# Out projections of a four-mixer block: from one fp32 product to three passes of split operands

## The chip, the cores and the metric

The kernel runs on one core of one Trainium2 chip. The metric is device microseconds of one execution. Three executions of the kernel before gave 1533.09, 1534.29 and 1536.28 us, a median of 1534.29 us.

## What is computed

The input is a sequence of 256 tokens with 1024 features. It runs through eight phases, each of the form x = x + f(rmsnorm(x)):

- **even**: a projection of 3584 columns, a causal depthwise convolution of 31 taps with layer norm and silu (features 0 to 511 of y), and softmax attention with 8 heads (features 512 to 1023 of y);
- **odd**: a projection, compressed, selected and windowed attention with gates (y 0 to 511) and sliding-window attention with sinks (y 512 to 1023);
- twice **ffn1, mix, ffn2**: a SwiGLU network with 2816 hidden features, a mixer, and another SwiGLU network. The mixer has an RWKV-7 recurrence with a group norm (y 0 to 511) and a chunked retention (y 512 to 1023).

Even, odd and the two mixers end with the same step, the subject of this document:

```python
x = x + einsum('bse,ed->bsd', y, w_out[layer])      # y: 256 x 1024, w_out: 1024 x 1024
# the end of the mixer's first half, ahead of that step
y = (y - mean) * rsqrt(var + LN_X_EPS) * ln_w + ln_b
y = (y + sum(r_h * k_h * r_k) * v_h) * g
```

## The kernel before, in words

**Tiles and passes.** All weights come as one stream of tiles of 128 x 1024 fp32 (512 KB), in the order of use, into a ring of six slots (`weight_ring`). A tile is either 128 columns of a weight over all 1024 inputs, or 128 rows of it (a row tile). The projections and the SwiGLU phases don't multiply in fp32: each operand a is split into hi = a rounded to fp32r (a copy on ScalarE, ACT) and lo = a - hi (a subtraction on VectorE, DVE). Then `three_passes` (L698 to L703) adds the products hi·hi, hi·lo and lo·hi in PSUM. `down` (L1009) does the same with row tiles, on the shape 128x128 by 128x512.

**The out projection** (L805, `out_projection`) is the exception: it takes y (`yT`, 128 features by 256 tokens for each of 8 groups k) and a row tile straight from the ring, and multiplies in fp32 at L815. For each of the eight row tiles it issues four matmuls of 128x128 by 128x512, one for each 128 tokens and each half of the 1024 output columns. They add up in PSUM banks 0 to 3. When the eighth is done, `add_to_x` (L1788) adds the four banks to x.

**Its inputs.** Attention phases make y in pairs of heads: `pair_done` on DVE (L1878 even, L1972 and L1975 odd) writes one group of `yT`, under the semaphore `pair_out`. The even phase's other half comes from the convolution: sums over features on TensorE (PE, L842 and L847), the centring (L1880), the square, the inverse root (L1400, L1401), a scaling (L1883), silu (L1458) and a product (L1885). In the mixer, the retention's half of y is written long before the end, and the recurrence's half last: group-norm sums (L1304, L1313), inverse root, then L2213, four scalings by ln_w and ln_b (L2215), the bonus (L2218) and the gate (L2219). The function `y_wait` holds PE in front of the group k that isn't made yet. The even phase and the mixer go through the groups 4 to 7 first and then 0 to 3; the odd phase goes through 0 to 7.

**What sets the order.** There is no planner: each engine (PE, ACT, DVE, and SP for the DMAs) has its own program, written out by hand in program order, and semaphores tie them together. An instruction that waits holds everything behind it on its engine. `attention` exists on all three engines with one step s for each pair of heads, plus some steps at the end to drain; `hook(s)` is where other work is put between the parts of a step. `ahead(n + 1)` (ACT L1363 ff., DVE L1766 ff.) splits the first two tiles of the next phase while the out projection runs. SP loads tile t + 6 into the slot of tile t as soon as that is free: after the lo part of a split tile is made (L618 ff.), or after PE's last matmul on an unsplit one (semaphore `w_used`, L625).

**Memory.** `arena` is scratch that shares its addresses with the hi and lo operands: six places for weight tiles (`w_hi`, `w_lo`), and `hT_hi`, `hT_lo`, the phase's normalised input. These are idle once a phase's last projection job is done.

## Time and profile before

| | |
|---|---|
| median of the runs | 1534.29 us (1533.09 to 1536.28) |
| the profiled execution, its own time | 1535.23 us |
| its span in the profile | 1533.4 us |
| PE busy | 1441.1 us, 94% of the span |
| DVE busy | 847.9 us, 55% |
| ACT busy | 689.1 us, 45% |
| matmuls of the out projections (L815) | 111.1 us of the busy time |
| mean granted clock of TensorE | 0.967 |

The profiled execution took 1535.23 us and its span is 1533.4 us, so 1.8 us lie around the span. A busy share says how full an engine is, not that it bounds: for that one reads, stage by stage, which wait ends last. A matmul's duration in a row (592 ns for L815) is its latency through a pipeline. What a run of matmuls costs is read from the time between its first and its last. One fp32 matmul leaves two records, so the 128 matmuls of L815 stand as 256.

### The profile page before, as it was taken

The numbers are of one execution on the slowest core, as the hardware profiler recorded it, in microseconds if no ns is written. First come the engines' busy times: TensorE is split into PE (matmuls) and PEld (weight loads), VectorE is DVE, ScalarE is ACT, GpSimd is POOL, SyncE is SP. The second block draws the span as 40 slices with busy tenths as digits, with TensorE's granted clock in tenths as the row PEclk, the third lists the DMA queues.
The fourth block names the chain that finished last, engine by engine and source line by source line (L and its number), as shares of the span: only waits on it lengthen the run. The fifth ranks groups of instructions, "written<-read, shape, count | busy, mean of one in ns | idle before, by whom it ended". The sixth has DMA issues, their size and how long they took to land.

```text
span 1533.4 us, 29116 instructions
## 1 busy us (share of the span) xinstructions
PE 1441.1 (94%) x11842; PEld 1264.9 (82%) x11842; DVE 847.9 (55%) x1218; ACT 689.1 (45%) x1044; POOL 9.9 (1%) x23
## 2 busy tenths in 40 slices
PE   6986997889999999999999999999999999999998
PEld 6974586665999989987599998999989988499997
DVE  4966526654555566744554546555557745455454
ACT  5452536554444446621444445444455531344443
POOL 1000000000000000000000000000000000000000
PEclk9996998899999999989999999999999989999999
DMA  8620544106655554400565554555545400465551
GB/s 328 207 83 18 189 167 176 56 1 195 202 178 194 175 167 163 138 3 3 165 208 188 182 187 152 204 186 183 189 154 168 150 15 3 150 207 177 192 179 67
DMA packets 62061, 228.14 MB, mean 149 GB/s; under 512 B 6928, under 2 KB 6928, under 8 KB 61728
## 3 DMA queue, kind: packets, MB, share of 16 engines
q1 hardware_dynamic: 60048, 218.14, 42.6%
q0 software_dynamic: 1936, 8.89, 1.7%
q8 instruction: 59, 0.97, 0.3%
q14 instruction: 18, 0.15, 0.0%
HBM read 225.95 MB, written 1.05 MB: 148 GB/s over the span
## 4 chain that ended last, share of the span: by engine, by line
PE 87%; DVE 5%; ACT 5%; issue 1%; DMA 1%; DVEq 0%; SPq 0%; ACTq 0%; PEldq 0%
PE PS L702 52%; PE PS L1009 15%; PE PS L815 7%; ACT arena L1347 1%; DVE w_lo L1764 1%; PE PS L1164 1%; PE PS L1196 1%; PE PS L1202 1%; PE PS L1211 1%; DVE arena L1857 1%; PE PS L1146 1%; PE PS L801 1%; PE PS L1141 1%; DVE x_res L1788 1%; DVE arena L1810 1%
## 5 line engine op out<-in xcount | busy, mean ns | idle before, releaser
L702 PE MATMUL PS<-hT_hi,w_hi 128*128 128x256 f32 x2136 | 612.2, 287 | 16.9 <-DVE w_lo L1764 10.6
L702 PE MATMUL PS<-hT_lo,w_hi 128*128 128x256 f32 x2136 | 608.7, 285 | 0.0
L702 PE MATMUL PS<-hT_hi,w_lo 128*128 128x256 f32 x2136 | 608.5, 285 | 0.0
L702 PEld LDWEIGHTS PS<-hT_hi,w_hi 128*128 128x128 f32 x2136 | 414.3, 194 | 24.8 <-issue 21.3
L702 PEld LDWEIGHTS PS<-hT_lo,w_hi 128*128 128x128 f32 x2136 | 414.3, 194 | 3.9 <-issue 0.7
L702 PEld LDWEIGHTS PS<-hT_hi,w_lo 128*128 128x128 f32 x2136 | 414.1, 194 | 0.0
L1984 DVE TENSOR_TENSOR w_lo<-weight_ring,w_hi 128x1024 fp32r<-128x1024 f32 x176 | 207.5, 1220 | 30.0 <-ACT w_hi L1548 30.0
L1990 DVE TENSOR_TENSOR w_lo<-weight_ring,w_hi 128x1024 fp32r<-128x1024 f32 x88 | 107.9, 1226 | 166.0 <-ACT w_hi L1557 166.0
L1548 ACT ACTIVATE w_hi<-weight_ring 128x1024 fp32r<-128x1024 f32 x176 | 175.6, 1044 | 39.5 <-DMA weight_ring<-in_stream 39.5
L1764 DVE TENSOR_TENSOR w_lo<-weight_ring,w_hi 128x1024 fp32r<-128x1024 f32 x107 | 126.1, 1221 | 54.6 <-ACT w_hi L1371 54.3
L1557 ACT ACTIVATE w_hi<-weight_ring 128x1024 fp32r<-128x1024 f32 x88 | 93.2, 1059 | 113.1 <-PE PS L1009 113.1
L1585 ACT ACTIVATE silu_gate<-PS 128x256 f32<-128x256 f32 x88 | 33.8, 384 | 239.3 <-PE PS L702 239.3
L1009 PE MATMUL PS<-w_hi,act_hi 128*128 128x512 f32 x352 | 138.0, 392 | 0.0
L1009 PE MATMUL PS<-w_hi,act_lo 128*128 128x512 f32 x352 | 138.0, 392 | 0.0
L1009 PE MATMUL PS<-w_lo,act_hi 128*128 128x512 f32 x352 | 136.9, 389 | 0.0
L2002 DVE TENSOR_TENSOR ffn_act<-silu_gate,PS 128x256 f32<-128x256 f32 x88 | 37.1, 422 | 143.7 <-ACT silu_gate L1585 143.7
L1371 ACT ACTIVATE w_hi<-weight_ring 128x1024 fp32r<-128x1024 f32 x107 | 107.1, 1052 | 18.6 <-DMA weight_ring<-in_stream 18.6
L815 PE MATMUL PS<-weight_ring,yT 128*128 128x512 f32 x256 | 111.1, 592 | 0.6 <-issue 0.6
L815 PEld LDWEIGHTS PS<-weight_ring,yT 128*128 128x128 f32 x256 | 48.7, 191 | 61.1 <-issue 60.9
L1009 PEld LDWEIGHTS PS<-w_lo,act_hi 128*128 128x128 f32 x352 | 66.1, 188 | 14.4
L1009 PEld LDWEIGHTS PS<-w_hi,act_hi 128*128 128x128 f32 x352 | 66.4, 189 | 11.6
L1009 PEld LDWEIGHTS PS<-w_hi,act_lo 128*128 128x128 f32 x352 | 66.4, 189 | 10.5
(275 smaller groups left out, 1353.3 us busy)
## 6 DMA issues: line engine op xcount, KB each, us to landing
weight_ring<-in_stream SPq DMA_DIRECT2D x411, 512.0 KB, 4.4
norm_gain<-in_gains_in POOLq DMA_DIRECT2D x9, 512.0 KB, 5.2
consts<-in_csts POOLq DMA_DIRECT2D x1, 1864.0 KB, 10.2
arena<-in_bias_in POOLq DMA_DIRECT2D x1, 1152.0 KB, 13.0
x_res<-in_x_in SPq DMA_DIRECT2D x2, 512.0 KB, 3.9
lora<-in_lora_in POOLq DMA_DIRECT2D x2, 512.0 KB, 5.7
x_out<-yT SPq DMA_DIRECT2D x2, 512.0 KB, 2.7
params<-in_params SPq DMA_DIRECT2D x1, 260.5 KB, 7.2
```

Source lines behind the costliest of these rows:

```text
L702: ins = pe.matmul(out, w[a], x[b], start=(start and i == 0), stop=(stop and i == 2))
L801: ins = pe.transpose(PS[:, 6 + e, c * P:(c + 1) * P], S[:, (s - 1) % 3, e, c * P:(c + 1) * P], ident)
L815: ins = pe.matmul(PS[:, 2 * t + half, :], YT[:, k, t * P:(t + 1) * P], w[:, half * 512:(half + 1) * 512], start=(i == 0), stop=(i == 7))
L1009: ins = pe.matmul(o, (Ah, Al)[x][:, s, t * P:(t + 1) * P], w[y][:, cols], start=(start and j == 0), stop=(stop and j == 2))
L1371: act.activation(Wh[:, q % RING], Wr[:, tile % NSLOT], ACT.Copy).then_inc(sem("tile_hi"), 1)
L1548: act.activation(Wh[:, 3 * (i % SS) + part], Wr[:, t % NSLOT], ACT.Copy)\
L1557: act.activation(Wh[:, 3 * (i % SS) + 2], Wr[:, t % NSLOT], ACT.Copy)\
L1585: act.activation(sg[:, s, :], PS[:, 4 + s, 0:T], ACT.Silu).then_inc(sem("silu_made"), 1)
L1764: dve.tensor_tensor(Wl[:, q % RING], Wr[:, tile % NSLOT], Wh[:, q % RING], ALU.subtract)\
L1984: dve.tensor_tensor(Wl[:, u], Wr[:, (tile0 + 3 * i + part) % NSLOT], Wh[:, u], ALU.subtract)\
L1990: dve.tensor_tensor(Wl[:, u], Wr[:, (tile0 + 3 * i + 2) % NSLOT], Wh[:, u], ALU.subtract)\
L2002: dve.tensor_tensor(aT[:, s, :], sg[:, s, :], PS[:, 4 + s, T:2 * T], ALU.mult)\
```

## The change

There are three parts.

1. **Three passes.** The out projection calls `three_passes` with y as the stationary and the row tile as the moving operand. New functions make the operands: `row_hi` (ACT, 128x1024) and `row_lo` (DVE, 128x1024) for a row tile, `y_hi` (ACT) and `y_lo` (DVE) for a group of y of 128x256 or 128x512. The split row tiles have two pairs of places (`OW[0][:, i % 2]`, `OW[1][:, i % 2]`), so `row_hi` of row i waits until PE is done with row i - 2 (`row_used`). The places lie where `w_lo` 4 and 5, `hT_hi` and `hT_lo` were; `yT_lo` lies on `yT` itself.
2. **Order.** `row_hi` and `row_lo`, `y_hi` and `y_lo` are written into the programs of ACT and DVE: rows 0 and 1 in the attention hooks (even, odd) or ahead of the last chain (mixer), rows 2 to 5 between the steps of the last chain, rows 6 and 7 behind the next phase's two split tiles. A ring slot of a row tile is free when its lo part is made, no longer after the matmuls. The odd phase takes the groups 4 to 7 first, as the others do.
3. **Last chains in halves.** In the even phase silu and the product are signalled and made in two halves. In the mixer ln_w, ln_b, the bonus and the gate are folded early into two factors (`output_factors`, in the inversion loop), and the last chain is three operations for each half of the features instead of seven for all of them.

```diff
...
-    return u + row_tiles(paired(wo[:512], 0), range(4)) + row_tiles(paired(wo[512:], 0), range(4)), 45
+    return u + row_tiles(paired(wo[512:], 0), range(4)) + row_tiles(paired(wo[:512], 0), range(4)), 45
...
-WOUT = {"even": (28, EVEN_OUT), "odd": (35, list(range(8))), "mix": (26, [4, 5, 6, 7, 0, 1, 2, 3])}
+WOUT = {"even": (28, EVEN_OUT), "odd": (35, EVEN_OUT), "mix": (26, EVEN_OUT)}
+Y_GROUPS = {"even": [(4, 5), (5, 6), (6, 7), (7, 8), (0, 2), (2, 4)], "odd": [(4, 6), (6, 8), (0, 1), (1, 2), (2, 3), (3, 4)],
+            "mix": [(4, 6), (6, 8), (0, 2), (2, 4)]}
...
+def outs_before(n):
+    kinds = [p[0] for p in PHASES[:n] if p[0] in WOUT]
+    return len(kinds), sum(len(Y_GROUPS[k]) for k in kinds)
...
+        with nc.sbuf_tensor("yT_lo", [P, KT, T], F32R) as YL:
+            pass
         YT = sb("yT", KT, T)
...
+        with nc.sbuf_tensor("out_operands", [P, ARENA], F32R) as rounded:
...
+        OUT_AT = PROJ_END - 6 * D
+        YH = rounded[:, OUT_AT:OUT_AT + KT * T].rearrange("p (k t) -> p k t", k=KT)
+        OW = [rounded[:, OUT_AT + 2 * D * (1 + i):OUT_AT + 2 * D * (2 + i)].rearrange("p (r n) -> p r n", r=2) for i in range(2)]
...
-                    else:
+                    elif i < WOUT[kind][0]:
                         used += 1
                         sp.wait_ge(sem("w_used"), used)
+                    else:
+                        sp.wait_ge(sem("row_lo"), 8 * outs_before(n)[0] + i - WOUT[kind][0] + 1)
...
-                first, order = WOUT[kind]
-                base = tile0 + first
-                for i, k in enumerate(order):
+                outs, groups = outs_before(n)
+                for i, k in enumerate(WOUT[kind][1]):
                     y_wait(k)
-                    tile_ready(base + i)
-                    w = unit(base + i).rearrange("p a b -> p (a b)")
+                    g = [a <= k < b for a, b in Y_GROUPS[kind]].index(True)
+                    pe.wait_ge(sem("y_lo"), groups + g + 1)
+                    pe.wait_ge(sem("row_lo"), 8 * outs + i + 1)
                     for t in range(NTT):
+                        y = [a[:, k, t * P:(t + 1) * P] for a in (YH, YL)]
                         for half in range(2):
-                            ins = pe.matmul(PS[:, 2 * t + half, :], YT[:, k, t * P:(t + 1) * P],
-                                            w[:, half * 512:(half + 1) * 512], start=(i == 0), stop=(i == 7))
+                            w = [a[:, i % 2, half * 512:(half + 1) * 512] for a in OW]
+                            ins = three_passes(PS[:, 2 * t + half, :], y, w, i == 0, i == 7)
                             if i == 7:
                                 ins.then_inc(sem("acc_made"), 1)
-                    if i < 7:
-                        ins.then_inc(sem("w_used"), 1)
-                pe.wait_ge(sem("acc_made"), 4 * n + 4)
-                pe.sem_inc(sem("w_used"), 1)
...
-                    if k == 0:
-                        pe.wait_ge(sem("y_conv_made"), 1)
...
+            def row_hi(n, i):
+                kind, l, tile0 = PHASES[n][:3]
+                tile = tile0 + WOUT[kind][0] + i
+                act.wait_ge(*loaded(tile))
+                if i >= 2:
+                    act.wait_ge(sem("row_used"), 6 * outs_before(n)[0] + i - 1)
+                act.activation(OW[0][:, i % 2], slot_of(tile), ACT.Copy).then_inc(sem("row_hi"), 1)
+            def y_hi(n, g):
+                lo, hi = Y_GROUPS[PHASES[n][0]][g]
+                act.activation(YH[:, lo:hi, :], YT[:, lo:hi, :], ACT.Copy).then_inc(sem("y_hi"), 1)
...
-                attention("even", lambda s: None)
+                attention("even", lambda s: row_hi(ph, s - 3) if s >= 3 else None)
+                for g in range(4):
+                    act.wait_ge(sem("pair_out"), g + 1)
+                    y_hi(ph, g)
                 act.wait_ge(sem("conv_centred"), 1)
                 act.activation(flat(convsq), flat(conv), ACT.Square).then_inc(sem("convsq_made"), 1)
+                row_hi(ph, 2)
                 act.wait_ge(sem("ln_sum_made"), 2)
                 inv_root(lnrs, PS[:, 4, T:2 * T], 1.0 / 512).then_inc(sem("lnrs_made"), 1)
+                row_hi(ph, 3)
+                act.preload_act_table(ACT.Silu)
                 act.wait_ge(sem("conv_scaled"), 1)
                 for c in range(4):
                     ins = act.activation(conv[:, c, :], conv[:, c, :], ACT.Silu, scale=par("a_ln_g", c, 1),
                                          bias=par("a_ln_b", c, 1))
-                ins.then_inc(sem("conv_act"), 1)
-            def odd_layer(jb0, hn0):
+                    if c % 2:
+                        ins.then_inc(sem("conv_act"), 1)
+                row_hi(ph, 4)
+                for h in range(2):
+                    act.wait_ge(sem("y_conv_made"), h + 1)
+                    y_hi(ph, 4 + h)
...
+                    elif s in (10, 11):
+                        row_hi(ph, s - 10)
...
                 attention("odd", hook)
+                act.wait_ge(sem("y_swa_made"), 1)
+                y_hi(ph, 0)
+                y_hi(ph, 1)
+                for j in range(4):
+                    act.wait_ge(sem("pair_out"), 4 + 4 + j + 1)
+                    y_hi(ph, 2 + j)
+                for i in range(2, 5):
+                    row_hi(ph, i)
...
+                row_hi(ph, 0)
+                for g in range(2):
+                    act.wait_ge(sem("y_ret_made"), 2 * l + 2)
+                    y_hi(ph, g)
+                row_hi(ph, 1)
...
+                row_hi(ph, 2)
                 act.wait_ge(sem("gn_sum"), 2 * l + 2)
                 inv_root(flat(aS), banks(6), 1.0 / HD, cst("lneps")).then_inc(sem("gn_rs_made"), 1)
+                row_hi(ph, 3)
+                row_hi(ph, 4)
+                for h in range(2):
+                    act.wait_ge(sem("y_mix_made"), 2 * l + h + 1)
+                    y_hi(ph, 2 + h)
...
+                    row_hi(n, 5)
                     ahead(n + 1)
+                    row_hi(n, 6)
+                    row_hi(n, 7)
...
+            def row_lo(n, i):
+                kind, l, tile0 = PHASES[n][:3]
+                dve.wait_ge(sem("row_hi"), 8 * outs_before(n)[0] + i + 1)
+                dve.tensor_tensor(OW[1][:, i % 2], slot_of(tile0 + WOUT[kind][0] + i), OW[0][:, i % 2], ALU.subtract)\
+                   .then_inc(sem("row_lo"), 1)
+            def y_lo(n, g):
+                lo, hi = Y_GROUPS[PHASES[n][0]][g]
+                dve.wait_ge(sem("y_hi"), outs_before(n)[1] + g + 1)
+                dve.tensor_tensor(YL[:, lo:hi, :], YT[:, lo:hi, :], YH[:, lo:hi, :], ALU.subtract)\
+                   .then_inc(sem("y_lo"), 1)
...
+                def with_rows(s):
+                    hook(s)
+                    if s >= 5:
+                        row_lo(ph, s - 5)
+                attention("even", lambda c, pv: dve.tensor_tensor(YT[:, c.tile, :], pv, ZB[:, c.j, :], ALU.mult), with_rows)
+                for g in range(4):
+                    y_lo(ph, g)
                 dve.wait_ge(sem("ln_sum_made"), 1)
                 dve.scalar_tensor_tensor(conv, rep(PS[:, 4, 0:T], 4), -1.0 / 512, conv, ALU.mult, ALU.add)\
                    .then_inc(sem("conv_centred"), 1)
+                row_lo(ph, 2)
                 dve.wait_ge(sem("lnrs_made"), 1)
                 dve.tensor_tensor(conv, conv, rep(lnrs, 4), ALU.mult).then_inc(sem("conv_scaled"), 1)
-                dve.wait_ge(sem("conv_act"), 1)
-                dve.tensor_tensor(YT[:, 0:4, :], conv, ZA, ALU.mult).then_inc(sem("y_conv_made"), 1)
-            def odd_layer(jb0, hn0):
+                row_lo(ph, 3)
+                for h in range(2):
+                    dve.wait_ge(sem("conv_act"), h + 1)
+                    cc = slice(2 * h, 2 * h + 2)
+                    dve.tensor_tensor(YT[:, cc, :], conv[:, cc, :], ZA[:, cc, :], ALU.mult)\
+                       .then_inc(sem("y_conv_made"), 1)
+                row_lo(ph, 4)
+                for h in range(2):
+                    y_lo(ph, 4 + h)
...
+                    elif s in (11, 12):
+                        row_lo(ph, s - 11)
                     elif s == 13:
                         dve.wait_ge(sem("z_gated"), 2)
                         dve.wait_ge(sem("pair_out"), 4 + 4)
-                        dve.tensor_tensor(flat(YT[:, 4:8, :]), flat(YT[:, 4:8, :]), flat(ZB), ALU.mult)
+                        dve.tensor_tensor(flat(YT[:, 4:8, :]), flat(YT[:, 4:8, :]), flat(ZB), ALU.mult)\
+                           .then_inc(sem("y_swa_made"), 1)
+                    elif s == 14:
+                        y_lo(ph, 0)
+                        y_lo(ph, 1)
...
+                for j in range(4):
+                    y_lo(ph, 2 + j)
+                for i in range(2, 5):
+                    row_lo(ph, i)
...
+                def output_factors(j):
+                    dve.wait_ge(sem("bonus_made"), l + 1)
+                    dve.wait_ge(sem("g_copied"), l + 1)
+                    dve.scalar_tensor_tensor(vS[:, j, :], vS[:, j, :], p_("ln_b", j), gS[:, j, :], ALU.add, ALU.mult)
+                    dve.tensor_scalar(gS[:, j, :], gS[:, j, :], p_("ln_w", j), None, ALU.mult)\
+                       .then_inc(sem("factors_made"), 1)
...
+                    if s < 4:
+                        output_factors(s)
...
+                row_lo(ph, 0)
+                y_lo(ph, 0)
+                y_lo(ph, 1)
...
+                row_lo(ph, 1)
+                row_lo(ph, 2)
+                dve.wait_ge(sem("factors_made"), 4 * l + 4)
                 dve.wait_ge(sem("gn_rs_made"), l + 1)
-                done.wait(done(dve.tensor_tensor(flat(Yl), flat(Yl), flat(aS), ALU.mult)))
-                for j in range(4):
-                    k = done(dve.tensor_scalar(Yl[:, j, :], Yl[:, j, :], p_("ln_w", j), p_("ln_b", j),
-                                               ALU.mult, ALU.add))
-                done.wait(k)
-                done.wait(done(dve.tensor_tensor(flat(Yl), flat(Yl), flat(vS), ALU.add)))
-                dve.tensor_tensor(flat(YT[:, 0:4, :]), flat(Yl), flat(gS), ALU.mult).then_inc(sem("y_mix_made"), 1)
+                for h in range(2):
+                    hh = slice(2 * h, 2 * h + 2)
+                    y = flat(Yl[:, hh, :])
+                    done.wait(done(dve.tensor_tensor(y, y, flat(aS[:, hh, :]), ALU.mult)))
+                    done.wait(done(dve.tensor_tensor(y, y, flat(gS[:, hh, :]), ALU.mult)))
+                    dve.tensor_tensor(flat(YT[:, hh, :]), y, flat(vS[:, hh, :]), ALU.add)\
+                       .then_inc(sem("y_mix_made"), 1)
+                    row_lo(ph, 3 + h)
+                for h in range(2):
+                    y_lo(ph, 2 + h)
...
+                    row_lo(n, 5)
                     ahead(n + 1)
+                    row_lo(n, 6)
+                    row_lo(n, 7)
```

## Rows read from the trace of the kernel before

**Rows 1.** The page: busy time of TensorE, and the chain by line.
```profile
PE 1441.1 (94%) x11842; PEld 1264.9 (82%) x11842; DVE 847.9 (55%) x1218; ACT 689.1 (45%) x1044; POOL 9.9 (1%) x23
...
PE PS L702 52%; PE PS L1009 15%; PE PS L815 7%; ACT arena L1347 1%; DVE w_lo L1764 1%; PE PS L1164 1%; PE PS L1196 1%; PE PS L1202 1%; PE PS L1211 1%; DVE arena L1857 1%; PE PS L1146 1%; PE PS L801 1%; PE PS L1141 1%; DVE x_res L1788 1%; DV
```

**Rows 2.** The chain in order of time: start, length, what.
```profile
268.00 1.75 ACT arena L1420 x8
...
333.10 1.04 DVE arena L1833 x2
...
340.97 26.00 PE PS L815 x60
...
385.90 2.75 PE PS L1009 x12
```

**Rows 3.** Windows: busy us of PE, PEld, DVE, ACT, POOL; granted clock; DMA.
```profile
141.00:145.00 4.00, 3.91 (x9) 3.09 (x10) 0.13 (x2) 0.00 (x0) 0.00 (x0) 0.53 0.00 0
...
298.00:302.00 4.00, 1.49 (x16) 0.77 (x14) 3.72 (x16) 0.47 (x1) 0.00 (x0) 0.97 0.78 260
302.00:305.00 3.00, 2.83 (x14) 2.50 (x16) 2.86 (x9) 1.25 (x4) 0.00 (x0) 0.50 0.02 8
...
337.00:341.00 4.00, 1.97 (x19) 1.16 (x17) 1.65 (x2) 1.96 (x3) 0.00 (x0) 1.00 0.00 0
...
341.00:368.70 27.70, 27.67 (x64) 12.02 (x64) 4.53 (x5) 4.38 (x5) 0.00 (x0) 1.00 0.43 133
```

**Rows 4.** Timeline of the first mixer's end: PE, then ACT, then DVE.
```profile
727.78 1.88 PE L1313 MATMUL PS<-arena,consts 128*128 128x512 f32 x4
729.50 24.20 PE L815 MATMUL PS<-weight_ring,yT 128*128 128x512 f32 x56
...
718.59 1.09 ACT L1706 ACTIVATE arena<-PS 128x512 f32<-128x512 f32 x2 [11.73 <-PE PS L1271]
...
729.70 1.11 ACT L1400 ACTIVATE arena<-PS,consts 128x1024 f32<-128x1024 f32 x1 [2.83 <-PE PS L1313]
...
740.15 1.06 ACT L1548 ACTIVATE w_hi<-weight_ring 128x1024 fp32r<-128x1024 f32 x1 [8.24 <-DMA weight_ring<-in_stream]
...
752.74 1.06 ACT L1347 ACTIVATE arena<-x_res 128x1024 f32<-128x1024 f32 x1 [6.79 <-DVE x_res L1788]
...
716.76 0.68 DVE L2180 TENSOR_TENSOR arena<-PS,arena 128x512 f32<-128x512 f32 x1
721.46 1.02 DVE L2207 TENSOR_TENSOR arena<-arena,PS 128x384 f32<-128x384 f32 x2 [4.02 <-PE PS L1298]
...
733.20 1.38 DVE L2215 TENSOR_SCALAR arena<-arena,params 128x256 f32<-128x256 f32 x4
...
735.88 1.23 DVE L2219 TENSOR_TENSOR yT<-arena 128x1024 f32<-128x1024 f32 x1
...
753.74 0.69 DVE L1788 SCALAR_TENSOR_TENSOR x_res<-PS,x_res 128x512 f32<-128x512 f32 x1 [0.17 <-PE PS L815]
```

**Rows 5.** Timeline of the second mixer's inversion loop, DVE.
```profile
1265.09 0.42 DVE L2160 TENSOR_TENSOR arena<-arena,PS 128x256 f32<-128x256 f32 x1 [0.75 <-PE PS L1211]
```

**Rows 6.** Timeline of the odd phase's last attention steps: ACT, then DVE.
```profile
331.38 0.81 ACT L1428 ACTIVATE lora<-PS 128x768 f32<-128x768 f32 x1
...
337.21 1.06 ACT L1536 ACTIVATE arena<-arena 128x1024 f32<-128x1024 f32 x1
338.18 0.79 ACT L1428 ACTIVATE lora<-PS 128x768 f32<-128x768 f32 x1
...
340.44 0.42 DVE L1975 TENSOR_TENSOR yT<-PS,arena 128x256 f32<-128x256 f32 x1 [0.91 <-PE PS L784]
```

**Rows 7.** Timeline of the even phase's end: PE, DVE and ACT.
```profile
140.61 0.42 DVE L1878 TENSOR_TENSOR yT<-PS,arena 128x256 f32<-128x256 f32 x1 [0.26 <-PE PS L776]
141.09 3.78 PE L842 MATMUL PS<-arena,consts 128*128 128x256 f32 x8 [0.53 <-DVE yT L1878]
...
155.74 2.07 ACT L1458 ACTIVATE arena<-arena,params 128x256 f32<-128x256 f32 x4
```

38 lines of the change are left out of this document (19 added, 19 removed).

## The prediction, made before the run

> **What bounds the kernel now.** I read the page first. TensorE is busy for 1441 of 1533 us, and the chain that ended last lies on it, with 7% in L815, the out projection's fp32 matmuls [rows 1]. A full engine proves nothing by itself, so next came the chain in order of time, around one out projection: 60 records without a gap in 26.00 us [rows 2]. PE bounds that stage, and less work on PE shortens it, as long as the work is fed. The windows give the clock: 1.00 over the odd phase's out projection, so the 2.4 GHz level [rows 3]. Last I read the timelines of the stage's three engines around it, since the change moves work to ACT and DVE.
>
> **The gross gain.** A fp32 matmul costs two records of 26.00/60 = 0.433 us, and a row tile (4 matmuls) 3.47 us, 8 of them 27.7 us. That is also the odd window of 27.70 us with 64 records [rows 2, 3]. Three passes of 128x128 by 128x512 in fp32r are what L1009 does: 12 matmuls in 2.75 us, 0.229 each [rows 2]. A row tile then costs 2.75 us and eight cost 22.0 us. So PE saves 5.7 us in each of the four out projections, 22.9 us in all. Now what eats into it.
>
> Beside the trace, the Trainium skill, FP8 and Floating Point Precision (TensorE Precision Notes), says that true fp32 takes four passes through the array. By that alone three passes would be 3/4 of 27.7, an estimate of 20.8 us. The row of L1009 gives 22.0, and it goes into the sum.
>
> **The feed.** Each row tile now needs an ACT copy (1.06 us, as the hi copy at 740.15) and then a DVE operation of 1.23 us (128x1024, as L2219) [rows 4]. A handover costs 0.04 us: L1313 ends at 729.66 and ACT starts at 729.70 [rows 4]. With two pairs of places, row i+2 is ready 1.06 + 1.23 + 3 x 0.04 = 2.4 us after row i is done, and row i+1 covers 2.75 us. It fits by 0.35 us, if ACT and DVE do nothing else. So each phase has to be followed in program order.
>
> **The mixer (twice).** Rows 0 and 1 and the retention's y: ACT is idle 11.73 us ahead of 718.59 and needs 2 x 1.06 + 2 x 0.55 = 3.2 us there. DVE's `row_lo(0)` and two `y_lo` (0.68 each, as L2180) take 2.6 us from 717.44 to 720.0. DVE is idle 4.02 us there, until 721.46 [rows 4]. Cost: nothing. Row 0 on PE starts at 724.35, as now (eight records of 0.43 ahead of 727.78), and ends at 727.1. The sums L1313 (1.88) run to 729.0 instead of 729.66. ACT's `row_hi(2)` fits ahead of them (727.1 to 728.2). Row 1 ends at 731.7, and row 2, whose lo is ready at 729.5, at 734.5. ACT's inverse root (two operations, 2.2 us) ends at 731.2. DVE then does half a chain (3 x 0.69 = 2.1, to 733.3) and `row_lo(3)` to 734.6: row 3 runs 734.65 to 737.4, a stall of 0.15. Then come the second half to 736.7, `row_lo(4)` to 737.9 and `y_lo(2)` to 738.6. Row 4 can't start before 738.65: a stall of 1.25. From there PE is continuous: DVE needs 1.23 for row 5, 2.46 for the next phase's two tiles and 1.23 for row 6 (739.3 to 744.15), and row 6 is due at 744.15. The next phase's tiles are loaded in time. Now the hi copy waits for a DMA until 740.15, whose slot came free with row 2 at 736.4 (3.75 us before); after the change it comes free with `row_lo(2)` and `row_lo(3)`, at 729.5 and 734.6. Row 7 ends at 749.65, against 753.70 (729.50 + 24.20) now [rows 4]: 4.05 us earlier.
>
> The tail gives some back. The four banks finish 0.69 us apart instead of 0.87, and the adds take 0.69 each. The second add, for which ACT's first square waits, now ends 0.96 us ahead of PE's end (752.74 against 753.70). It will end 0.6 ahead. The last add ends as late after PE's end as it does now, 0.73 us (753.74 + 0.69), but ACT's two token tiles follow each other without a gap, so the next phase starts 0.36 us later against PE's end [rows 4]. Four times: 1.4 us.
>
> `output_factors` adds a 128x256 operation with three inputs (0.42) and one of 1.38/4 = 0.35 [rows 4, 5] in each of four rounds of the inversion loop. DVE is idle 0.75 us there [rows 5], so 0.77 us hides but for some 0.02 to 0.1 us. I take 0.15 us for each mixer; without that cover it would be 4 x 0.77 = 3.1. The chain gets shorter by the four scalings and the half that is signalled early, but `y_mix_made` is at 737.1 now and PE wants group 0 at 739.8 (729.50 + 24 x 0.43) [rows 4]: that gain is spent on the feed.
>
> Each mixer: 4.05 - 0.36 - 0.15 = 3.55 us. Two: 7.1 us.
>
> **The odd phase.** The hooks of steps 10 and 11 put `row_hi` ahead of the PT copy (331.38) and `row_lo` ahead of the normalisation on DVE [rows 6]. ACT: `row_hi(0)` to 332.4, the PT copy to 333.25, the exponentials of step 11 (eight records, 1.75 and a handover [rows 2]) to 335.1, `row_hi(1)` to 336.15. At step 12 DVE waits for that, does `row_lo(1)` to 337.4 and normalises (1.04 [rows 2] behind three small operations of some 0.2) to 339.0, and PE transposes (0.9) to 339.95. ACT's last PT copy slips from 338.18 to 339.95 (now it waits for the silu from 337.21). Then the two `y_lo` of step 14 stand ahead of the last `pair_done`: it ends at about 343.1 instead of 340.86, and PE's row 0 starts at 343.2 instead of 340.97, 2.2 us late [rows 2, 6]. The rows then run continuously but for 0.55 at row 6: behind `row_lo(5)` (356.55), DVE has the two tiles (359.0) and `row_lo(6)` (360.2), and row 6 is due at 359.7. End: 343.2 + 22.0 + 0.55 = 365.75 against 368.7. Less the tail: 2.95 - 0.36 = 2.6 us gained.
>
> **The even phase.** Here the last `pair_done` on DVE is what PE waits for, until 141.09 [rows 7]. `row_lo(0)` and `row_lo(1)` come in steps 5 and 6, ahead of the last two `pair_done`: 2 x 1.23, less 0.26 of idle, puts it at 143.15 and L842 at 143.2, 2.1 us late. L842 takes 3.78 us, rows 0 and 1 end at 152.5, the second sums (8 records of half that size at the full clock, 1.89) at 154.4, row 2 at 157.15. Inverse root, `row_hi(3)`, the table load and the wait for the scaling bring silu to 157.7 instead of 155.74. `row_lo(3)` is ready at 157.9: a stall of 0.75. silu (2.07) ends at 159.8, then `row_hi(4)`, `row_lo(4)` and `y_lo(4)` to 162.85: a stall of 2.2. End at 173.9 against 174.06. With the tail, the even phase loses 0.2 us.
>
> **The sum.** 7.1 + 2.6 - 0.2 = 9.5 us. The profiled execution took 1535.23 us, so 1525.7 by it; it lies 0.94 us above the median of 1534.29. The change applied to the median gives **1524.8 us**.
>
> **What the trace of before doesn't show.** (1) A DVE subtraction or an ACT copy that reads the ring beside fp32r matmuls of 512 columns: L1009's stage does that, so no loss; at the other end 10% more on 1.23 and 1.06 would use 0.23 of the 0.35 us of margin. (2) The handover through three engines in each row: 0.04 each by the row above, up to 0.2 (the gap of DVE behind L815 is 0.17 [rows 4]), so a row between 2.75 and 2.9 us: 0 to 24 x 0.15 = 3.6 us lost. I take 0, since 0.35 of margin stands against it. (3) The clock.
>
> **Rivals.**
>
> *The clock falls at the start of row 0.* Between 298 and 302 PE was busy for 1.49 of 4 us, with its work at the front, and the next window was granted 0.50, the 1.2 GHz level; 337 to 341, with 1.97 of 4, kept 1.00 [rows 3]. After the change the last steps of the odd phase are stretched, with about 3.5 us busy in 8 and gaps near 1 us. In the even phase L842 already runs at the low level (0.53), behind a gap that grows from 0.53 to 2.6 us. If one row runs at the low level it costs 2.75 us more; in both phases 5.5: 1527.5 to 1530.3. For it: the gaps grow. Against it: none of the odd phase's is as long as the 2.5 us in which PE was idle in that window.
> The Trainium skill, TensorE: Matmul & The Clock Gate (Part 1), says that half rate is the idle state and that sustained activity lifts it. By that rule the even phase's row 0 still starts at the full clock, since L842 runs ahead of it; the trace agrees.
>
> *The feed sets the pace, and the kernel gets slower.* Place: `row_lo` behind `row_hi` behind `row_used`, 32 rows. If a row takes p instead of 2.75 us, the loss is 32(p - 2.75), which eats the 9.5 us at p = 3.05, a chain of 2.4 us lengthened by 0.65. At p = 3.3, 17.6 us are lost and the time is 1542. For it: the margin of 0.35, and ACT and DVE have other work between the rows in every phase. Against it: the durations of both are read in the SwiGLU stage, where they run as densely.
>
> *The hidden gain.* The late starts cost more than I worked out: the even and the odd phase lose 3 us each beyond it (one more `row_lo` plus one stall of 2 us), and each mixer's stall at row 4 is 2.5. Then 1533. For it: the four delays add up through three engines. Against it: every step has its row.
>
> *It doesn't do what it says.* Nothing in the diff leaves the fp32 path in place, so no chance for that.
>
> **Chances.** Forecast 1524.8 (1521 to 1528): 0.60. Clock: 0.17. Hidden gain: 0.13. Feed, slower: 0.10. What a measurement can tell from no change is about 0.2%, 3.1 us. Faster by more than that: 0.60 + 0.17 and a little of the hidden gain, 0.80. Same: 0.12. Slower: 0.08. The range that holds 8 in 10 reaches from 1520.5, with shorter stalls at row 4, to 1531, through most of the clock's case.
>
> **What would show it.** L815's place taken by 384 fp32r matmuls in L702's helper, 12 in 2.75 us. In each mixer one PE stall of about 1.2 us ahead of group 0, waited for by `y_lo`, and the end 4 us earlier. In the odd phase row 0 late by 2.2 us; in the even phase L842 at about 2.1 us late, with the end where it was. ACT's square 0.6 ahead of PE's end. Wrong would be: rows more than 2.85 us apart without a step of the last chain between them (the feed), a granted clock under 0.9 within an out projection, or an inversion loop over 1 us longer.

## The result, and the profile after

| | before | after | ratio (95% interval) |
|---|---|---|---|
| first comparison, median of 4 runs each | 1534.03 us (1533.09 to 1536.28) | 1525.46 us (1523.79 to 1527.44) | 0.9947 (0.9926 to 0.9968) |
| same kernel again, 6 runs (18 of before) | 1534.32 us | 1524.73 us (1523.66 to 1526.84) | 0.9942 (0.9927 to 0.9956) |

The forecast was 1524.8 us, faster by 9.5. The change is worth 8.6 and 9.6 us in the two comparisons. The profiled execution took 1526.04 us (span 1524.3).

The page after: busy time of the engines, the chain that ended last by engine, and the group of out projection matmuls with both operands in `out_operands`.

```profile
PE 1422.4 (93%) x11970; PEld 1288.3 (85%) x11970; DVE 898.0 (59%) x1285; ACT 729.9 (48%) x1096; POOL 9.9 (1%) x23
...
PE 84%; DVE 8%; ACT 5%; issue 1%; DMA 1%; DVEq 0%; SPq 0%; ACTq 0%; PEldq 0%
...
L719 PE MATMUL PS<-out_operands 128*128 128x512 f32 x256 | 84.0, 409 | 6.1 <-DVE yT_lo L1851 3.0
```

TensorE is busy 18.7 us less [rows 1] and the span is 9.1 us shorter; VectorE is busy 50 us more, and its share of the chain has gone from 5 to 8%. That fits a change that takes work off the bound and pays half of it back in waits. The waits can be read one by one. The timeline of PE around the out projections, only the lines with an idle time ahead: even phase, odd phase, first mixer.

```profile
143.59 2.93 PE L858 MATMUL PS<-arena,consts 128*128 128x256 f32 x6 [2.44 <-DVE yT L1955]
...
158.91 0.70 PE L719 MATMUL PS<-out_operands 128*128 128x512 f32 x2 [0.74 <-DVE out_operands L1844]
...
163.58 0.73 PE L719 MATMUL PS<-out_operands 128*128 128x512 f32 x2 [1.67 <-DVE yT_lo L1851]
...
344.14 0.70 PE L719 MATMUL PS<-out_operands 128*128 128x512 f32 x2 [1.45 <-DVE yT L2068]
...
361.46 0.70 PE L719 MATMUL PS<-out_operands 128*128 128x512 f32 x2 [0.40 <-DVE out_operands L1844]
...
735.81 0.70 PE L719 MATMUL PS<-out_operands 128*128 128x512 f32 x2 [0.23 <-DVE out_operands L1844]
739.50 0.73 PE L719 MATMUL PS<-out_operands 128*128 128x512 f32 x2 [0.69 <-DVE yT_lo L1851]
```

Every stall that the prediction named is there. It had put 2.1 us ahead of the even phase's first sums (L858, L842 before [rows 7]), 0.75 and 2.2 behind it, 0.55 at row 6 of the odd phase, 0.15 and 1.25 in the mixer. Only their sizes differ.

The chain in order of time through the odd phase's out projection (start, length, what):

```profile
341.74 0.64 ACT out_operands L1395
342.38 0.02 issue
342.41 0.56 DVE yT_lo L1851
342.96 0.06 issue
343.02 0.68 DVE yT_lo L1851
343.70 0.35 DVE yT L2068
344.05 0.09 issue
344.14 11.37 PE PS L719 x48
355.50 0.02 issue
355.52 0.02 ACTq L1390
355.54 0.04 issue
355.59 1.07 ACT out_operands L1391
356.65 0.02 issue
356.68 1.23 DVE out_operands L1844
357.90 2.27 DVE w_lo L2081 x2
360.17 1.15 DVE out_operands L1844
361.32 0.14 issue
361.46 3.71 PE PS L719 x15
```

Its upper part is what holds row 0: two low parts of y on VectorE (L1851) ahead of the last normalised pair (L2068). Its lower part holds row 6: the next phase's two tiles (L2081) ahead of row 6's low part. The granted clock is 1.00 through this stretch of the odd phase, the 2.4 GHz level [rows 3]:

```profile
337.00:341.00 4.00, 1.98 (x17) 1.12 (x14) 3.31 (x8) 3.62 (x4) 0.00 (x0) 1.00 0.53 179
341.00:345.00 4.00, 2.17 (x16) 1.46 (x17) 3.30 (x8) 2.82 (x7) 0.00 (x0) 1.00 0.00 0
345.00:367.00 22.00, 21.61 (x94) 16.80 (x92) 11.72 (x13) 9.81 (x10) 0.00 (x0) 1.00 0.48 153
```

In the even phase it is lower. There row 0 starts at 146.81, and the clock is at 0.50 (the 1.2 GHz level) until 148.95:

```profile
144.00:147.00 3.00, 3.00 (x9) 2.37 (x8) 0.87 (x3) 0.00 (x0) 0.00 (x0) 0.50 0.71 232
147.00:149.00 2.00, 2.00 (x6) 1.52 (x6) 1.22 (x1) 0.33 (x1) 0.00 (x0) 0.51 0.04 16
149.00:152.00 3.00, 3.00 (x15) 2.45 (x14) 0.00 (x0) 1.71 (x2) 0.00 (x0) 1.00 0.00 0
```

In the kernel before, row 0 starts at 144.66 and the clock rises at 144.74. The first mixer's row 0 has 1.6 us at 0.50 too (724.23 to 725.81).

### The profile page after: what moved, and what is told of

It reads as the page before. It is cut to its first block, busy times and chain, and to the rows that moved or that the text cites. A ratio compares the mean times of both kernels' runs of the same rounds, so it can differ in the third digit from the quotient of the medians.

```text
span 1524.3 us, 29548 instructions
## 1 busy us (share of the span) xinstructions
PE 1422.4 (93%) x11970; PEld 1288.3 (85%) x11970; DVE 898.0 (59%) x1285; ACT 729.9 (48%) x1096; POOL 9.9 (1%) x23
## 3 DMA queue, kind: packets, MB, share of 16 engines
HBM read 225.95 MB, written 1.05 MB: 149 GB/s over the span
## 4 chain that ended last, share of the span: by engine, by line
PE 84%; DVE 8%; ACT 5%; issue 1%; DMA 1%; DVEq 0%; SPq 0%; ACTq 0%; PEldq 0%
PE PS L719 56%; PE PS L1023 15%; ACT arena L1357 1%; DVE w_lo L1822 1%; PE PS L707 1%; DVE arena L1928 1%; PE PS L1178 1%; PE PS L1210 1%; PE PS L1216 1%; DVE out_operands L1844 1%; DVE x_res L1859 1%; PE PS L1160 1%; PE PS L781 1%; DVE arena L1881 1%; PE PS L1155 1%
## 5 line engine op out<-in xcount | busy, mean ns | idle before, releaser
L2081 DVE TENSOR_TENSOR w_lo<-weight_ring,w_hi 128x1024 fp32r<-128x1024 f32 x176 | 207.3, 1220 | 0.0
L719 PE MATMUL PS<-out_operands 128*128 128x512 f32 x256 | 84.0, 409 | 6.1 <-DVE yT_lo L1851 3.0
L719 PEld LDWEIGHTS PS<-out_operands 128*128 128x128 f32 x256 | 47.6, 191 | 23.2 <-issue 9.3
```

Of the source, the lines that this page charges most:

```text
L719: ins = pe.matmul(out, w[a], x[b], start=(start and i == 0), stop=(stop and i == 2))
L2081: dve.tensor_tensor(Wl[:, u], Wr[:, (tile0 + 3 * i + part) % NSLOT], Wh[:, u], ALU.subtract)\
```

## The experiments

**Which part of the change brings it.** The first kernel is the one before with the mixers' part of the shorter chains alone:

```
+ output_factors(s) in rounds 0 to 3 of the inversion loop
- y = Yl * aS (128x1024); Yl * gS; + vS;  y_mix_made once
+ for h in range(2): the three operations on a half; y_mix_made twice
```

> The kernel before with the third part of the change alone, in the mixers: output_factors in the inversion loop, and the last chain in halves with two signals. Fp32 out projection as before. Theory: the chain was hidden (y_mix_made at 737.1 against a need at 739.8) and the factors hide in DVE's 0.75 us of idle, so 1534.3, between 0.5 less and 1 more. Rival: the shorter chain carries part of the measured gain by itself, 1532 or less. Second rival: the factors stand in the way of the inversion loop, 4 x 0.77 us in each mixer, 1540.

Measured: 1534.71 us (12 runs), ratio 0.9996 (0.998 to 1.0012). The mixers' chain alone gives nothing that can be measured: a shorter chain beside a busy PE is hidden. The gain is the split matmuls' (or needs them). The even phase's halves weren't tried alone.

**The changed kernel again**, as the base of the comparisons:

> The changed kernel once more, for a narrower interval and a second trace. My reading of its first trace: the out projections and their starts gained what was worked out (mixers about 3.2 us each of the expected 3.55, even phase +0.5 instead of +0.2, odd phase 2.4 instead of 2.6), while two stretches at the 1.2 GHz level moved: one came in at the start of the first SwiGLU phase (1.9 us lost, row 0 there took 5.75 + 1.9 us), one fell away at the start of the second mixer (1.7 us gained). If these come by chance, this trace shows them at other phase starts, and the median stays at 1525.5 (1524 to 1527). Rival: the change itself moved the clock (longer gaps ahead of the first SwiGLU phase), then the same two places show it again.

Measured: 1524.73 us (1523.66 to 1526.84, 6 runs), as expected. Of the two places, the start of the first SwiGLU phase is low in the second trace again, and that of the second mixer, which was low for 3.4 us only in the first trace, is low for 6.8 us. So one place speaks for the rival, that the change itself moved the clock, and one for chance. The count over all traces (below) bears on it.

**The work on rows 0 and 1 ahead of the attention's last steps.** It is moved behind them, or to where PE doesn't wait:

```
- even: row_lo(0), row_lo(1) in steps 5 and 6      + behind the attention
- odd, ACT: row_hi(0), row_hi(1) in steps 10, 11   + step 9; between the two y_hi
- odd, DVE: row_lo in steps 11, 12; y_lo(0), y_lo(1) in step 14
+ row_lo(0) in step 13; y_lo(0), row_lo(1), y_lo(1) behind the attention
```

> The changed kernel, with the row tiles' and y's splits moved behind the last pair in the even and odd phases: row_lo(0), row_lo(1) after the attention on DVE in the even phase; in the odd phase row_hi(0) in step 9, row_lo(0) in step 13, row_hi(1), row_lo(1) and the first two y_lo after the last pair_done. Theory: the late starts of L858 (2.0 us) and of row 0 (2.4 us) were these operations standing ahead of pair_done, so 4.4 us come back: 1521.1 (1520 to 1522.5). Rival (hidden): the work only moves and row 0 or row 1 waits for it instead; then 1525.

Measured: 1518.57 us (1516.99 to 1521.8), ratio 0.9898 (0.9882 to 0.9915), 6.2 us less than the changed kernel and 1.4 below the range expected. In the even phase L858 starts 2.07 us behind the start of the last attention step's matmuls (L793), as in the kernel before; in the changed kernel it was 3.99. So 1.9 us of the even phase's delay is the two low parts. In the odd phase I count from the fourth-last step's matmuls of PT (the tile `lora`) to row 0: 11.3 us before, 13.4 after, 12.0 here. The gain in medians is larger than these 1.9 + 1.4 us. Another 0.7 is in the even phase's rows 0 and 1: up to the second sums they take 6.0 us for 6.7, since the clock is at 0.50 for the first 0.5 us of them and not for 2.1. The other 2.2 aren't shown to be the change's. The even phase's stretch from its first normed operation to row 0 is 130.2 us here and 134.0 to 134.2 in four traces with the changed kernel's code, but 132.1 in three others with the same code ahead of row 0, so they may be scatter.

**The next phase's tiles between rows 6 and 7.** Both engines do one of the two tiles ahead of row 6 and one behind it (`ahead(n + 1, 0)`, row 6, `ahead(n + 1, 1)`, row 7).

> The changed kernel, with the next phase's two split tiles put one behind row 5 and one behind row 6, instead of both between 5 and 6. Theory: only the odd phase's row 6 has a stall there (0.4 us), so 1525.1, no more than 0.7 less than the changed kernel. Rival (feed sets the pace in rows 5 to 7 of every phase): 2 to 4 us less.

Measured: 1526.37 us (1516.93 to 1529.77, 7 runs), ratio 0.9943 (0.992 to 0.9965): no difference. The stall at row 6 of the odd phase is gone (its rows take 22.5 us for 23.1), but 0.6 us is under the scatter.

**Is the feed hidden, and by how much?** Three kernels ask it. The first leaves one pass out of each product, which makes the rows cheaper for PE while the feed stays:

```
- three_passes(PS[...], y, w, i == 0, i == 7)
+ for m, (a, b) in enumerate(((0, 0), (0, 1))): pe.matmul(PS[...], y[a], w[b], ...)
```

> The changed kernel with two of the three passes of each out projection product: y high by row high and y high by row low; the third, y low by row high, is left out, and with it that part of the product (y low is still made and waited for). A row tile then costs TensorE 8 instead of 12 matmuls, 2.75 x 8/12 = 1.83 us, 0.92 us less; four projections of 8 rows make 29.3 us of TensorE work less. My theory, corrected after the first traces: the chain that feeds a row (row high copy 1.06 us, row low subtraction 1.22 us, and the handovers, about 2.2 to 2.6 us a row with two pairs of places) is just under 2.75 us, so that it is hidden now and becomes the bound as soon as the rows are cheaper: rows 2 to 7 then take 2.3 to 2.6 us each instead of 1.83, and a projection saves 2 x 0.92 for its first two rows and at most 6 x 0.4 for the rest, less what the late groups of y hold (even and mixers nothing before row 4): some 2 to 4 us a projection, 8 to 16 in all: 1510 to 1517 us. Rival 1, TensorE alone sets the pace: 29 us less, 1496. Rival 2, the feed sets the pace already in the changed kernel: nothing is saved behind row 1, about 1522 to 1525, and the rows of the trace stand 2.75 us apart as before.

Measured: 1521.73 us (1517.63 to 1523.5), ratio 0.9927 (0.9905 to 0.9948). 29.3 us of PE's work left the kernel and only 3 us of time. The time is above the 1510 to 1517 expected and next to the second rival's 1522; the distance of the rows, 2.32 us for that rival's 2.75, speaks against it. The timeline of PE in its odd phase, rows 0 and 1, then 2 and 3, then 4 and 5:

```profile
341.22 3.89 PE L835 MATMUL PS<-out_operands 128*128 128x512 f32 x16 [1.44 <-DVE yT L2070]
345.87 3.91 PE L835 MATMUL PS<-out_operands 128*128 128x512 f32 x16 [0.75 <-DVE out_operands L1846]
350.50 3.91 PE L835 MATMUL PS<-out_operands 128*128 128x512 f32 x16 [0.73 <-DVE out_operands L1846]
```

ScalarE and VectorE in the same timeline:

```profile
348.04 1.06 ACT L1393 ACTIVATE out_operands<-weight_ring 128x1024 fp32r<-128x1024 f32 x1 [1.77 <-PE PS L835]
349.13 1.23 DVE L1846 TENSOR_TENSOR out_operands<-weight_ring,out_operands 128x1024 fp32r<-128x1024 f32 x1 [1.60 <-ACT out_operands L1393]
```

Two rows every 4.64 us, and PE waits ahead of each pair. Half of the pair's 3.9 us is row 2, so by this estimate it ends at 347.82; ScalarE starts row 4 0.22 behind it and takes 1.06; VectorE starts at 349.13, takes 1.23, and PE starts 0.14 later: 2.68 us (4.64 - 1.95 = 2.69). Neither engine is full: both stand idle for over 1.5 us ahead of these rows. What binds is the cycle of a place, with two places.

The third pair of places tests that. `OUT_AT` moves down by two row tiles, `i % 2` becomes `i % 3`, and row i waits for the matmuls of row i - 3:

```
- OUT_AT = PROJ_END - 6 * D              + OUT_AT = PROJ_END - 8 * D
- act.wait_ge(row_used, 6 * outs + i - 1)  + act.wait_ge(row_used, 5 * outs + i - 2)
```

> The kernel with two passes (y low by row high left out of the product) and three pairs of places instead of two. My theory: what held the rows of the two-pass kernel at 2.32 us is the cycle of a place (copy, subtraction, handovers, matmuls), not ScalarE or VectorE (1.06 and 1.22 us a row): with three places that cycle gives (2.69 + 1.95) / 3 = 1.55 us a row, below the 1.95 of the matmuls, so the odd phase's rows 2 to 7 stand 1.95 us apart; up to 0.37 x 6 = 2.2 us less there than with two pairs, 1 us in the other phases, where the rest waits for the late groups of y: 1517 us beside 1521.7. Rival, the engines' own queues (the copy and the subtraction in turn, other work between them) set 2.32 us: no change in the pitch, 1521.7.

Measured: 1517.17 us (1511.0 to 1519.28), ratio 0.9893 (0.9877 to 0.9909), 4.6 us less than two passes with two pairs. ScalarE's copies of rows 3 to 5 in the odd phase now stand 1.93 and 1.81 us apart, at the pace of PE; the waits behind each pair are gone:

```profile
340.58 1.06 ACT L1393 ACTIVATE out_operands<-weight_ring 128x1024 fp32r<-128x1024 f32 x1 [2.55 <-PE PS L835]
342.51 1.06 ACT L1393 ACTIVATE out_operands<-weight_ring 128x1024 fp32r<-128x1024 f32 x1 [0.86 <-PE PS L835]
344.32 1.06 ACT L1393 ACTIVATE out_operands<-weight_ring 128x1024 fp32r<-128x1024 f32 x1 [0.75 <-PE PS L835]
```

Shown, then: the cycle of the two places set 2.32 us, not an engine's queue. The third kernel comes from the other side and lengthens the feed of the full three passes: the low part of rows 2 to 7 is made twice. An earlier forecast for it, made for a first form that gave no result, was 3.4 us a row and 1541 us (1536 to 1546).

> The changed kernel with VectorE's low part of row tiles 2 to 7 made twice, the second behind the first (1.22 us and a step of some 0.05 us more for each). My theory, sized on the kernel with two passes (in the odd phase a row's matmuls end 2.69 us before the next pair of rows begins, 4.64 less 1.95): with two pairs of places the copy, the subtraction and their handovers of a row must fit into the 2.75 us of the row ahead, and take 2.69, so the room is 0.06 us. Made twice they take 3.96: two rows then take 3.96 + 2.75 = 6.71 us in place of 5.5, 3.36 us a row, 0.6 us more on each of rows 2 to 7, 3.6 us in the odd phase and 2 to 4 in the others (VectorE's last chains in the mixers and the even phase queue behind the longer parts): 14 us in all, 1539 us (1535 to 1543). Rival, the room is the 0.35 us of the prediction: 0.45 a row, 3 us a projection, 1536 us and a pitch of 3.2 us. Rival, the room is over a microsecond: 2.75 us a row as before, under 1528.

Measured: 1545.59 us (1544.75 to 1547.49), ratio 1.0075 (1.0061 to 1.0089), slower than the kernel before. The timeline of PE in its odd phase:

```profile
355.77 0.70 PE L719 MATMUL PS<-out_operands 128*128 128x512 f32 x2 [1.05 <-DVE out_operands L1847]
362.61 0.70 PE L719 MATMUL PS<-out_operands 128*128 128x512 f32 x2 [1.05 <-DVE out_operands L1847]
370.05 0.70 PE L719 MATMUL PS<-out_operands 128*128 128x512 f32 x2 [1.65 <-DVE out_operands L1847]
```

The pair of rows 2 and 3 takes 6.84 us, where 6.71 had been worked out; the room is as small as the theory says. The next pair takes 7.44, with the next phase's two tiles in VectorE's way. The time is 6 us above the expected 1539. The stalls ahead of y's late groups grew too (1.95 in each mixer against 0.69), and, in this execution, the odd phase ran at a granted clock of 0.50 from 338 us until row 1 (windows, columns as in [rows 3]):

```profile
341.00:344.00 3.00, 2.10 (x12) 1.44 (x10) 1.35 (x2) 2.25 (x4) 0.00 (x0) 0.50 0.31 126
344.00:348.00 4.00, 3.36 (x15) 1.99 (x12) 3.06 (x7) 2.03 (x6) 0.00 (x0) 0.50 0.02 4
```

How the 6 us divide between these two isn't shown. The low clock is the prediction's rival, at its place. The trace with two passes and three pairs has it too (0.50 to 0.58 from 334 to 341 us); the code ahead of row 0 is that of the changed kernel, which kept 1.00 there in both of its traces. And the trace of lo_later has it: 0.50 over the first 6.2 us of the odd phase's rows, which take 25.9 us in it and 23.1 in the changed kernel.

**Three pairs for three passes, and the mixer's end in another order.**

> The changed kernel with the low parts of rows 0 and 1 behind the attention's own steps (as in lo_later) and three pairs of places instead of two, so that a row's high copy waits for the matmuls of three rows before. My theory: two pairs are just enough; what three can give is the stall ahead of row 3 or 6 (0.74 in the even phase, 0.39 in the odd one, 0.23 in each mixer), 1.6 us at most, and nothing in the pace of the rows: 1517.5 us beside 1518.6 for lo_later. Rival, the feed set the pace of the rows (2.78 us against 2.75 of matmuls): with three pairs the rows stand 2.72 to 2.75 apart, another 0.03 x 24 = 0.7 us. If two pairs cost much more than the trace shows, 1514 or less.

Measured: 1518.19 us (1514.7 to 1521.64), ratio 0.9896 (0.9873 to 0.9918), beside 1518.57: nothing that can be measured. The stall at row 6 of the odd phase is gone, that of 0.74 in the even phase and that of 0.23 in each mixer stayed: they aren't a matter of places. The rows stand 2.77 to 2.78 us apart as before, so that pace is PE's. Where PE takes 2.78 us, two pairs are enough.

> three_later with the mixer's end in another order: ScalarE copies y group 2 ahead of rows 4 and 5, VectorE makes row 3 low, y group 2 low and row 4 low between the two halves of the last chain, then row 5 low, then y group 3 low. My theory: the stall ahead of the mixers' row 4 (0.69 us each, for the low part of y) goes, if the second half of the chain and the group behind it are still in time for row 6 (by the durations it ends 1.5 us ahead): 1.4 us less than three_later, 1516.1 us. Rival: row 5's low part comes late instead and holds row 5 by as much as was won, no difference; or group 3 is late at row 6, up to 1 us a mixer slower.

Measured: 1521.14 us (1519.51 to 1524.96), ratio 0.9926 (0.9903 to 0.995). The stall of 0.69 in the mixers is gone, one of 0.38 has come at row 6; the second mixer takes 184.5 us in both traces. From row 0 to the next phase each mixer gains 0.4 us (26.7 for 27.0), far under the scatter. No gain in the time, where 1516.1 was expected; whether it loses stays open, the intervals overlap.

**What scatters the runs.** The first normed operation of each phase gives the phases' starts. SwiGLU phases take 193, some 193.5 or 195.2 us, with the same code, and the windows behind the start tell why: the granted clock stays at 1.00, is at 0.50 for 3.4 us (a short fall) or for 6.8 us (a long one). Of the seven phase starts behind the first, three had a long fall before and three after (others: four with the chain only, three in lo_later, one in the trace of the kernel with tiles between the rows). The changed kernel's first trace has three short falls besides, the kernel before none. Two starts of the same trace of lo_later, both phases SwiGLU, the first (behind an out projection) high, the second (behind another SwiGLU phase) low:

```profile
366.00:370.00 4.00, 2.62 (x16) 1.68 (x16) 3.77 (x7) 3.54 (x9) 0.71 (x2) 1.00 0.72 243
370.00:374.00 4.00, 3.94 (x33) 3.97 (x34) 4.00 (x5) 3.97 (x4) 0.00 (x0) 1.00 0.44 135
937.00:941.00 4.00, 3.28 (x16) 2.40 (x16) 3.32 (x6) 2.89 (x8) 0.53 (x1) 0.69 0.42 151
941.00:945.00 4.00, 3.81 (x18) 3.85 (x19) 4.00 (x6) 3.98 (x5) 0.00 (x0) 0.50 0.30 116
```

Both stand behind the same wait of PE for the normed rows, 2.0 us. Does the wait let the clock fall? A kernel fills it:

```
  def transposes_in(n):
+     if n:
+         for _ in range(2):
+             pe.matmul(PS[:, 7, :], ident, CSTt[:, 0:512], start=True, stop=True)
```

> lo_later (1518.6 us) with two matmuls more of 128x512 in fp32 at the head of each phase but the first (consts by consts into a bank that the transposes overwrite; no result uses them), 1.74 us of TensorE work in the 2.0 us in which it waited for the normed rows. In the traces so far two to four of the eight phases behind the first begin at a granted clock of 0.50 and are 2 us longer than those that begin at 1.00, another set of them in each execution, always behind this wait. Theory A, the idle time in this wait is what lets the clock fall: no phase, or hardly one, begins at 0.50, the runs lie within 1 us of one another and the median is 3 x 2 = 6 us lower, 1512.6 us. Theory B, the wait has no part in it (what falls is set by the work ahead or by the short transposes behind): two to four phases begin at 0.50 as before and the time stays, 1518.6 (or 0.2 us a phase more where the extra matmuls end late, 1520).

Measured: **1513.48 us** (1513.09 to 1514.4), ratio 0.9865 (0.985 to 0.988), the best of all kernels here. All seven starts are at 1.00, all four SwiGLU phases take 192.9 us, and the runs lie within 1.3 us. The median is 5.1 us under that of lo_later, for 6 expected. PE at the same start as above (matmuls into a bank that is overwritten, then the transposes):

```profile
934.32 1.96 PE L704 MATMUL PS<-consts 128*128 128x512 f32 x4
...
937.73 1.32 PE L710 MATMUL PS<-consts,yT 128*128 128x128 f32 x8 [0.21 <-DVE yT L1808]
```

Theory A holds. The Trainium skill, TensorE: Matmul & The Clock Gate (Part 1), calls half rate the idle state; that a wait of 2.0 us ahead of the transposes is enough is what these traces add.

Did the change bring falls of its own? The eleven traces without the two matmuls have 77 phase starts, with 33 long falls and 21 short ones. Behind a SwiGLU phase PE waits 2.03 us or more with either code, and every start falls: 6 of 6 in the traces of before and of the chain only, 27 of 27 in the other nine. Behind an out projection PE waits 1.68 us in those two traces and 1 of 8 starts falls; in the nine others the wait is 2.0 to 2.6 us, and 20 of 36 fall, 11 of them long. So by this count the longer wait that the change makes there brings falls. No run alters that wait alone, so this isn't shown, but the rival of after_again is likely right in part.

The same two matmuls in the kernel before and in the changed one:

> The kernel before with the two idle-time matmuls at the head of each phase but the first, as in kept_busy. In its profile three phases begin at a granted clock of 0.50. If these starts are the same burden before and after the change, 3 x 2 = 6 us go: 1528 us, with a spread of 1 to 2 us. If the kernel before has fewer of them than the changed one, less goes, 1530 or more, and part of what the change can give was hidden by the clock.

> The changed kernel with the same two matmuls at the head of each phase but the first. Theory: 1519 us (1525 less 3 x 2), so that beside before_busy the change gives what it gives without them, 9 us (ratio 0.994), and the forecast's sum of 9.5 can be held against two kernels that don't scatter with the clock. By kept_busy (1513.5) and what lo_later gave (6.2 us) it comes to 1519.7. Rival: the change's own count of low starts is larger, and the pair differs by more, 12 us. Phase by phase, all ffn phases 192.9 us in both, odd 194.6 and 192.3, mixers 190 and 186.5 less what the clock gives (about 188 and 184.5).

Measured: 1526.17 us (1520.84 to 1532.76, 12 runs), ratio 0.9957 (0.9941 to 0.9972), and 1519.81 us (1517.81 to 1520.64, 5 runs), ratio 0.9912 (0.9895 to 0.9929). Of the seven phase starts none is low in either trace. The changed kernel gains 4.9 us by it and scatters over 2.8. The kernel before gains 8 and still scatters over 12: its odd phase takes 189.2 us in this trace and 194.6 in the profile of before, and the difference (5.4 us) has arisen ahead of the fourth-last step of the attention, which the change doesn't touch. The mean granted clock over that stretch is 0.92 in the profile of before and 0.93 here, which accounts for 1 to 2 us at most; the rest is open. The pair differs by 6.4 us, less than the 9 expected; with intervals of 2.4 and 2.6 us to each side this tells little against 9.

## Why the prediction was right, and where it was off

- **Gross gain.** 5.7 us a projection. In the odd phase rows 1 to 5 start at 346.98, 349.75, 352.54, 355.33 and 358.10, 2.78 us apart, for 2.75. So 0.03 a row, 1 us in all, went unseen. It stays with three pairs of places, so it is PE's own and not the feed.
- **The feed.** It was right that the feed is hidden, and the size was wrong: 2.69 us, not 2.4. The term that was off is "a handover costs 0.04 us", taken three times. One between ScalarE and VectorE does cost 0.03, but from PE's last matmul to ScalarE it is 0.22, and from VectorE to PE 0.14. The margin is 0.06 us of each row, not 0.35. The forecast came out because 2.69 is still under 2.75: the slower rival was nearer than its chance of 0.10, since a feed longer by more than 0.06 us a row would have shown, as the doubled low part does. The prediction had allowed for up to 0.2 us a handover in its list of what the trace of before doesn't show, and had set that term to nothing by the margin of 0.35.
- **The mixers.** Forecast 3.55 us each, all of it behind the start of row 0: 3.7 gained there, 0.15 lost ahead. Behind it the second trace gained 3.1 twice (30.1 before, 27.0 after, to the next phase's first normed operation). The stalls are 0.23 and 0.69 for 0.15 and 1.25, so they aren't what is missing; 0.2 us is the rows' pace, and the rest isn't located. In the first trace the first mixer gained only 2.4, with its row 0 at the low clock. Ahead of row 0 nothing was to be gained, but the mixers are 2.6 and 1.6 us shorter there (161.8 and 161.5 before, 159.2 and 159.9 in the second trace), with low stretches of the same lengths (6.8 and 10.2 us) in all four. In the first, 1.9 of the 2.6 lie in the inversion loop. There PE waits in the kernel before for nothing that the profile shows:

```profile
692.43 1.01 PE L1211 MATMUL PS<-arena 64*64 64x32 f32 x53 [0.37 <-issue]
...
700.37 0.30 PE L1196 MATMUL PS<-arena 64*64 64x32 f32 x2 [1.15 <-issue]
```

  The trace with the chain only has such waits too, and both traces of the changed kernel have none. So it isn't the factors that remove them; what does stays open. Nor is it a gain to count on: with PE kept busy the stretches ahead of row 0 are 157.9 and 160.0 before and 157.5 and 160.1 after, with the clock low at other places.
- **The odd phase.** Forecast: row 0 late by 2.2, 2.6 gained. By the distance to that step of the attention, 11.3 and 13.4, it is late by 2.1. From row 0 to the next phase's first normed operation it is 28.5 before and 24.2 after, 4.3 gained there for 4.8 forecast, so 2.2 net. Close; the pace is 0.2 of what is missing.
- **The even phase.** Forecast 0.2 lost. From the start of the last attention step's matmuls to the next phase's first normed operation it is 35.8 and 36.5 us: 0.7 lost. The delay (1.9 for 2.1) and the two stalls (0.74 and 1.67 for 0.75 and 2.2) are where they were put, and give 0.7 back. What was missing is the low clock over row 0's first 2.1 us, which costs half of them, 1.1 us by this estimate.
- **The tail.** Forecast 0.36 a phase. PE's wait ahead of the transposes behind the odd phase is 1.68 us before and 2.01 after, 0.33, and the same at the first mixer:

```profile
752.89 1.38 PE L707 MATMUL PS<-consts,yT 128*128 128x128 f32 x6 [2.01 <-DVE yT L1804]
```

- **The factors** in the inversion loop: 0.15 a mixer can't be told from nothing (chain_only, within 0.2%).
- **The sum.** The number is right partly by luck. In the second trace, whose span is 11.5 us shorter than in the profile of before, the four out projections gained 11.3 us from row 0 on (0.8, 4.3, 3.1 and 3.1), where the forecast's terms make 14.1 (1.9, 4.8, 3.7 and 3.7). The late starts cost 3.9 (1.9 and 2.0) for 4.3. What made up for it was in no term: 4.2 us ahead of row 0 in the mixers. The mechanism (less work on PE, a hidden feed, late starts and stalls where they were put) is what the traces show; the gross gain of the stretches was some 3 us too large.
- **The clock.** This rival came true in part, and so did one of the prediction's signs of being wrong, a granted clock under 0.9 within an out projection. In the even phase row 0 starts at 0.50 in both traces of the changed kernel, for 2.1 and 2.4 us. The prediction had row 0 start at the full clock, since L842 runs ahead of it. Behind a wait of 0.53 us the clock does rise 3.7 us from the start of L842 before and 3.8 from that of L858 in lo_later; behind the wait of 2.44 in the changed kernel it rises 5.4 us from it, when row 0 has begun. At row 0 of the odd phase these two traces kept 1.00. The rival's price, 2.75 us for a whole row at the low level, was too high for what came (1.1 us, and 0.7 in one mixer), so the forecast held. The falls at phase starts are the larger part. Behind SwiGLU phases they were there before the change. Behind out projections they came more often after it, and the forecast priced the later start at 0.36 us a phase and no fall. They are part of what makes the runs of one kernel differ by 3 to 13 us, more than most terms.

## What to carry to other kernels

Count a feed through double buffers by its cycle, the matmuls of one place included, and take each handover from the row of the engine pair that makes it: 0.03 us between two engines is not 0.22 behind a matmul. Work of the next stage that is put ahead of the last step that PE waits for costs its own duration, whatever is idle later; put it behind. And where PE waits 2 us for a short chain, look at the granted clock behind it: filling the wait with matmuls that nobody reads was worth 5 us here, as much as half of the change. Check a sum of terms place by place and not by its total: here two errors of about 3 and 4 us cancelled.

## What the runs showed of the hardware

- A matmul of 128x128 by 128x512 costs 0.433 us a record in fp32 (two records each) and 0.229 in fp32r, at a granted clock of 1.00.
- With a doubled low part PE had 1.05 us of wait per pair of rows and the clock stayed at 1.00; behind a wait of 2.0 us or more ahead of the transposes it fell at 53 of 69 phase starts, and behind one of 1.68 us at 1 of 8. A fall of 6.8 us cost about 2.2 us (SwiGLU phases of 195.2 for 192.9), one of 3.4 us about 0.5. With the wait filled, none of 21 fell in the traces of three kernels.
- Why a start behind an out projection falls in one execution and not in another stays open.
